# A layer in one core: modulation in plain f32 by column groups, x loaded first, values in 512 columns

## The reference

```python
mod_ctx = jax.nn.silu(c_ctx)[None, :] @ w_mod[l] + b_mod[l]      # 1024 -> 6 * 1024
mod_lat = jax.nn.silu(c) @ w_mod[l] + b_mod[l]
...
shift1, scale1, gate1, shift2, scale2, gate2 = [m[:, None, :] for m in jnp.split(mod, 6, axis=-1)]
h = _rmsnorm(x, g_norm1) * (1 + scale1) + shift1
proj = h @ w_in + b_in
q_raw, k_raw, v_raw, o_raw, gates, u_pool, g_a, g_b = jnp.split(proj, split_at, axis=-1)
y_a, C, n, m = _mlstm_branch(q_raw, k_raw, v_raw, o_raw, gates, gn_gain, C0, n0, m0)
...
x = x + gate1 * (merged @ w_out)
h2 = _rmsnorm(x, g_norm2) * (1 + scale2) + shift2
x = x + gate2 * _hier_moe(h2, ...)
```

## Time and profile before

| | before |
|---|---|
| median of 3 runs | 1079.4 us (1077.72 to 1080.03) |
| the profiled execution | 1075.08 us |
| its span, first to last instruction | 1073.3 us |
| mean granted clock of PE, as a share of 2.4 GHz | 0.965 |
| PE busy | 993.5 us, 93% |
| DVE busy | 634.5 us, 59% |
| ACT busy | 515.3 us, 48% |
| POOL busy | 133.7 us, 12% |

### The profile page before, as it was taken

How to read it: one execution, slowest core, us unless ns; L and a number is a source line. 1 busy time by engine, 2 the same in 40 slices (tenths; PEclk the granted TensorE clock), 3 DMA queues, 4 the chain that set the end, 5 groups by cost and what they waited for, 6 DMA issues and landing times.

```text
span 1073.3 us, 14490 instructions
## 1 busy us (share of the span) xinstructions
PE 993.5 (93%) x5934; PEld 873.2 (81%) x5934; DVE 634.5 (59%) x774; ACT 515.3 (48%) x656; POOL 133.7 (12%) x135
## 2 busy tenths in 40 slices
PE   6899999999999999999999999982999999999970
PEld 2378888899888989999998998882788888888860
DVE  0645643323476768232116444536699999999987
ACT  2353343413556664222214123223578787878763
POOL 3000000000110100896000000001011111111010
PEclk9899999999999999999999999985899999999995
DMA  9734434421334324231221124521899999999955
GB/s 348 312 118 176 176 135 184 157 105 40 89 93 119 92 57 156 107 126 66 79 79 67 56 75 182 229 94 64 360 379 416 422 411 417 413 419 416 396 231 203
DMA packets 36066, 216.41 MB, mean 202 GB/s; under 512 B 4352, under 2 KB 4800, under 8 KB 15520
## 3 DMA queue, kind: packets, MB, share of 16 engines
q1 hardware_dynamic: 27024, 180.23, 43.2%
q0 software_dynamic: 8112, 32.53, 8.7%
q10 hardware_dynamic: 864, 2.73, 0.6%
HBM read 200.68 MB, written 14.79 MB: 201 GB/s over the span
## 4 chain that ended last, share of the span: by engine, by line
PE 84%; DVE 6%; DMA 5%; ACT 2%; issue 1%; SPq 0%; DVEq 0%; POOL 0%; ACTq 0%; POOLq 0%
PE ps L1476 81%; DMA rowA<-yscr 2%; DMA raw<-in_wst 1%; PE ps L1857 1%; DVE xr L1454 1%; DVE rowB L1451 1%; DVE hn L958 1%; PE ps L1875 1%; DMA xg<-h2scr,slot_rows 1%; DVE hlo L971 0%; DVE hn L976 0%; DVE xr L1458 0%; PE ps L1808 0%; DMA yscr<-yb,slot_rows 0%; PE ps L1740 0%
## 5 line engine op out<-in xcount | busy, mean ns | idle before, releaser
L932 DVE TENSOR_TENSOR wlo<-raw,whi 128x2048 fp32r<-128x2048 f32 x37 | 86.1, 2329 | 146.9 <-ACT whi L579 146.9
L1476 PE MATMUL ps<-hhi,whi 128*128 128x320 f32 x672 | 153.9, 310 | 1.7 <-ACT gF L616 1.7
L1476 PE MATMUL ps<-hlo,whi 128*128 128x320 f32 x672 | 153.1, 309 | 0.0
L1476 PE MATMUL ps<-hhi,wlo 128*128 128x320 f32 x672 | 153.0, 309 | 0.0
L1476 PEld LDWEIGHTS ps<-hhi,whi 128*128 128x128 f32 x672 | 112.6, 188 | 4.9 <-ACT gF L616 2.0
L1476 PEld LDWEIGHTS ps<-hhi,wlo 128*128 128x128 f32 x672 | 112.4, 188 | 0.0
L1476 PEld LDWEIGHTS ps<-hlo,whi 128*128 128x128 f32 x672 | 112.4, 188 | 0.0
L579 ACT ACTIVATE whi<-raw 128x2048 fp32r<-128x2048 f32 x37 | 70.5, 1907 | 85.9 <-PE ps L1476 83.7
L1351 DVE TENSOR_TENSOR wlo<-raw,whi 128x2048 fp32r<-128x2048 f32 x32 | 72.6, 2289 | 5.4 <-ACT whi L859 5.3
L1351 DVE TENSOR_TENSOR olo<-raw,ohi 128x2048 fp32r<-128x2048 f32 x32 | 72.5, 2288 | 4.5 <-ACT ohi L859 4.5
L859 ACT ACTIVATE whi<-raw 128x2048 fp32r<-128x2048 f32 x32 | 61.3, 1919 | 18.3 <-PE ps L1476 18.3
(11 more groups left out here) (331 smaller groups left out, 2253.1 us busy)
## 6 DMA issues: line engine op xcount, KB each, us to landing
raw<-in_wexp SPq DMA_DIRECT2D x64, 1024.0 KB, 8.8
raw<-in_wst SPq DMA_DIRECT2D x60, 1024.0 KB, 5.0
eraw<-in_wexp SPq DMA_DIRECT2D x32, 1024.0 KB, 7.5
nm<-negscr POOLq DMA_DIRECT2D x8, 640.0 KB, 7.0
wib<-wiscr POOLq DMA_DIRECT2D x8, 512.0 KB, 6.1
xT<-in_x SPq DMA_DIRECT2D x4, 640.0 KB, 10.8
xr<-in_xt SPq DMA_DIRECT2D x1, 2560.0 KB, 10.9
h2scr<-ht ACTq DMA_DIRECT2D x5, 512.0 KB, 3.0
```

Of the source, the lines that this page charges most:

```text
L932: dve.tensor_tensor(lo[:, :], raw[s][:, :], f32(hi[:, :]), ALU.subtract)\
L1476: return nc.tensor.matmul(out, lhsT, rhs, start=start, stop=stop)
```

## The change

- `in_wst` is laid out anew for the modulation chunks and for the values. A modulation chunk of the start-up now holds four k tiles of 512 columns, these being shift and scale of two k tiles; so a pair of chunks (`i`, 0 to 3) completes shift1 and scale1 of k tiles 2i and 2i + 1.
- `mod_half` multiplies such a chunk straight from `raw`, in plain f32, in the start-up and in the query/key stage alike: four matmuls, one for each k tile, each with a stationary operand of 32 columns (`csil`, zeros beyond the first two) and with its own 32 rows of the result. `mod_columns` adds the four rows together as it transposes, by a constant with ones at rows 0 and 1 of each 32.
- The second modulation needs no split on ACT and DVE, and `wx`, `wxl`, `ch4`, `cz4` go. `split_no` gives the new count of splits.
- SP issues x first, then chunks; the eight small loads go to ACT's queue. `vb` is loaded after chunk AT_QK + 2.
- PE makes the sums of squares before any modulation matmul. DVE multiplies x by rstd at once, then takes the k tiles two by two as each pair's shift and scale arrive; query chunk 0 is split in the last of these turns.
- The gate matmuls of a k tile and those of query blocks 0 and 1 stand in one loop over k tiles, so the loop of 8 turns has no blocks left in turn 0, and waits there for the gates' copies.
- The values are made in two groups of 512 channels, each from two chunks of four k tiles: `value_block` multiplies 12 times 512 columns, and DVE adds 512 columns at a time, after the second chunk.
- POOL's memset of `Vt` and its loads wait for the last modulation chunk instead of `m_used`.

The diff, cut to its core:

```diff
+def split_no(c):
+    return 1 + (c - AT_QK) // 3 if c < AT_V else N_QK + 1 + c - AT_V
...
-        mrow1 = at("mrow1", 92, [4, 8 * P])
+        mrow1 = at("mrow1", TMP + 5, [P, 4, 512])
...
-        wx = at("wx", 152, [P, CH], F32R), at("wxl", 160, [P, CH], F32R)
-        QH, QL = whi + [wx[0]], wlo + [wx[1]]
-        ch4 = at("ch4", 177.75, [P, KT, 4], F32R)
-        cz4 = at("cz4", 178, [P, KT, 4], F32R)
+        QH, QL = whi, wlo
+        csil = at("csil", 176.75, [P, KT, 32])
...
-            smalls = [(cst[:, :], cst_d), (cin[:, :, :], c_d), (col[:, :], col_d),
-                      (wgr[:, :, :], wg_d), (bg[:, :], bg_d), (m0[:, :], m0_d),
-                      (wr[:, :, :], wr_d), (br[:, :], br_d)]
-            assert len(smalls) == N_SMALL
-            for dst, src in smalls:
-                sp.dma_start(dst, src).then_inc(d_const, 16)
+            for k in range(0, KT, 2):
+                sp.dma_start(xT[:, k:k + 2, :], x_d[:, k:k + 2, :]).then_inc(d_x[k // 2], 16)
...
-                if c < 4:
-                    sp.dma_start(xT[:, 2 * c:2 * c + 2, :], x_d[:, 2 * c:2 * c + 2, :])\
-                      .then_inc(d_x[c], 16)
-                elif c == 4:
+                if c == AT_QK + 2:
...
+            for dst, src in smalls:
+                act.dma_start(dst, src).then_inc(d_const, 16)
...
+            for i in range(4):
+                chunk_used(act, 2 * i + 1)
+                act.activation(mrow1[:, i, :], ps[:, 2 + i, :], ACT.Copy).then_inc(s_mrow, 1)
+                if i == 3:
+                    split_hi(AT_QK, QH[0])
+                for k in (2 * i, 2 * i + 1):
+                    act.wait_ge(s_hn, k + 1)
+                    act.activation(hhi[:, k, :], hn[:, k, :], ACT.Copy).then_inc(s_hhi, 1)
...
             for j in range(N_QK):
-                c = AT_QK + 3 * j
                 if j:
                     act.wait_ge(q_used, j)
-                split_hi(c + 1, QH[(j + 1) % 2])
-                if j:
-                    act.wait_ge(m_used, 2 * j)
-                split_hi(c + 2, QH[2])
+                split_hi(AT_QK + 3 * j + 3, QH[(j + 1) % 2])
                 block_qk(2 * j)
-                if j < N_QK - 1:
-                    act.wait_ge(m_used, 2 * j + 1)
-                    split_hi(c + 3, QH[(j + 1) % 2])
-                else:
-                    act.wait_ge(m_used, 2 * j + 1)
-                    split_hi(AT_V, QH[0])
                 block_qk(2 * j + 1)
                 mod_row2(j)
...
+            dve.wait_ge(s_rstd, 1)
+            for k in range(KT):
+                st.on(dve.tensor_tensor(hn[:, k, :], xT[:, k, :], rstd[:, :], ALU.mult))
...
+            for i in range(4):
+                dve.wait_ge(s_modT, i + 1)
+                both = mod[:, 0:16, :].rearrange("p (s k) c -> p s k c", s=2)[:, :, 2 * i:2 * i + 2, :]
+                bias = col[:, B_MOD:B_MOD + 16].rearrange("p (s k) -> p s k", s=2)
+                st.do(dve.tensor_tensor(both, ps[:, 0, 448 + 8 * i:456 + 8 * i].rearrange(
+                    "p (s k c) -> p s k c", s=2, c=2), by(bias[:, :, 2 * i:2 * i + 2].unsqueeze(3),
+                                                          [P, 2, 2, 2]), ALU.add))
+                st.do(dve.scalar_tensor_tensor(
+                    gain[:, 2 * i:2 * i + 2, :], mod[:, 8 + 2 * i:10 + 2 * i, :], 1.0,
+                    by(col[:, G_1 + 2 * i:G_1 + 2 * i + 2].unsqueeze(2), [P, 2, 2]), ALU.add, ALU.mult))
+                for k in (2 * i, 2 * i + 1):
+                    for c, a, b in ((0, 0, TC), (1, TC, T)):
+                        ins = dve.tensor_scalar(hn[:, k, a:b], hn[:, k, a:b], gain[:, k, c:c + 1],
+                                                mod[:, k, c:c + 1], ALU.mult, ALU.add)
+                    ins.then_inc(s_hn, 1)
+                if i == 3:
+                    split_lo(AT_QK, QH[0], QL[0])
+                for k in (2 * i, 2 * i + 1):
+                    input_lo(k)
 
...
             def splits_lo(j):
                 c, o = AT_QK + 3 * j, (j + 1) % 2
-                split_lo(c + 1, QH[o], QL[o])
-                split_lo(c + 2, QH[2], QL[2])
-                if j < N_QK - 1:
-                    split_lo(c + 3, QH[o], QL[o])
-                else:
-                    split_lo(AT_V, QH[0], QL[0])
+                split_lo(c + 3, QH[o], QL[o])
...
-            def value_rows(c, t):
-                n = c * NT + t
-                dve.wait_ge(v_ready, n + 1)
-                dve.tensor_tensor(Vt[:, t, 2 * c:2 * c + 2, 0:DH], ps[:, (n + 2) % 6, 0:2 * P].rearrange(
-                    "p (v n) -> p v n", n=P), vb[:, 2 * c * P:2 * (c + 1) * P].rearrange(
+            def value_rows(g, t):
+                u = g * NT + t
+                dve.wait_ge(v_ready, (2 * g + 1) * NT + t + 1)
+                dve.tensor_tensor(Vt[:, t, 4 * g:4 * g + 4, 0:DH], ps[:, (u + 2) % 6, :].rearrange(
+                    "p (v n) -> p v n", n=P), vb[:, 512 * g:512 * (g + 1)].rearrange(
                         "p (v n) -> p v n", n=P), ALU.add).then_inc(v_free, 1)
...
-            def mod_chunk(slot, use, out, c2):
-
-
-                pe.wait_ge(raw_full[slot], (use + 1) * 16)
-                for k in range(KT):
-                    last = mm(out, csil[:, k, 2 - 2 * c2:6 - 2 * c2],
-                              raw[slot][:, k * 2 * P:(k + 1) * 2 * P],
-                              k == 0 and c2 == 0, k == KT - 1 and c2 == 1)
+            def mod_half(c, kh, bank):
+
+                slot = raw_slot(c)
+                pe.wait_ge(raw_full[slot], (raw_use(c) + 1) * 16)
+                for kk in range(4):
+                    last = nc.tensor.matmul(
+                        ps[32 * kk:32 * kk + 32, bank, :], csil[:, 4 * kh + kk, :],
+                        raw[slot][:, kk * 512:(kk + 1) * 512], start=kh == 0, stop=kh == 1,
+                        tile_position=(0, 32 * kk))
                 last.then_inc(raw_free[slot], 1)
+
+            def mod_columns(rows, out):
+                for b in range(4):
+                    last = mm(out[:, 2 * b:2 * b + 2], rows[:, b * P:(b + 1) * P],
+                              cst[:, C_CMB:C_CMB + 2], True, True)
+                last.then_inc(s_modT, 1)
 
...
-            last.then_inc(s_modT, 1)
+            pe.wait_ge(s_csil, 3)
+            square_sums(hn, s_sum1, s_ssq)
+            for i in range(4):
+                mod_half(2 * i, 0, 2 + i)
+                mod_half(2 * i + 1, 1, 2 + i)
+                if i == 0:
+                    pe.wait_ge(s_rstd, 1)
+                pe.wait_ge(s_mrow, i + 1)
+                mod_columns(mrow1[:, i, :], ps[:, 0, 448 + 8 * i:456 + 8 * i])
 
             pe.wait_ge(s_wgl, 1)
+            chunk_split(AT_QK)
             for k in range(KT):
                 pe.wait_ge(s_hlo, k + 1)
                 last = three([(ps[0:GP, 6 + a, 0:HALF], cut_half(a)) for a in range(2)],
                              wgh[:, k, :], wgl[:, k, :], hhi[:, k, :], hlo[:, k, :],
                              k == 0, k == KT - 1)
-            last.then_inc(s_gps, 1)
+                if k == KT - 1:
+                    last.then_inc(s_gps, 1)
+                for b in range(2):
+                    o = (b * KT + k) * P
+                    last = three([(ps[:, 2 * b + a, 0:HALF], cut_half(a)) for a in range(2)],
+                                 QH[0][:, o:o + P], QL[0][:, o:o + P], hhi[:, k, :], hlo[:, k, :],
+                                 k == 0, k == KT - 1)
+                    if k == KT - 1:
+                        last.then_inc(q_ready, 1)
 
...
-            def mod_half(j, kh):
-                w = 2 if kh else (j + 1) % 2
-                chunk_split(AT_QK + 3 * j + 1 + kh)
-                if kh == 0:
-                    pe.wait_ge(s_mrow, 2 + j)
-                for kk in range(4):
-                    k = 4 * kh + kk
-                    mm(ps[0:4, 6, :], ch4[:, k, :], QH[w][:, kk * 512:(kk + 1) * 512], k == 0, False)
-                    last = mm(ps[0:4, 6, :], cz4[:, k, :], QL[w][:, kk * 512:(kk + 1) * 512], False,
-                              k == KT - 1)
-                last.then_inc(m_used, 1)
-
-            def mod_columns(i):
-                pe.wait_ge(s_mrow, 3 + i)
-                if i:
-                    pe.wait_ge(m_done, i)
-                for b in range(4):
-                    last = mm(ps[:, 7, 2 * b:2 * b + 2], mrow[:, b * P:(b + 1) * P],
-                              cst[0:4, C_CMB:C_CMB + 2], True, True)
-                last.then_inc(s_modT, 1)
-
-            pe.wait_ge(s_gate, 2)
-            pe.wait_ge(s_ch, 4)
             for j in range(N_QK):
-                block_q(j, 0)
                 if j:
-                    mod_columns(j - 1)
-                mod_half(j, 0)
-                block_q(j, 1)
+                    block_q(j, 0)
+                    pe.wait_ge(m_done, j - 1)
+                    pe.wait_ge(s_mrow, 4 + j)
+                    mod_columns(mrow, ps[:, 7, 0:8])
+                else:
+                    pe.wait_ge(s_gate, 2)
```

(60 more changed lines are left out.)

74 lines of the change are left out of this document (29 added, 45 removed).

## The result

The changed kernel takes 1084.38 us (median; 1081.38 to 1087.06), the kernel before 1079.24 us in the same rounds (1074.87 to 1080.22): ratio 1.0052, 95% interval 1.0033 to 1.0071, so it is slower by 5 us, and the forecast was 1086.7 us. The profiled execution took 1087.06 us, its span 1084.8 us.

What follows compares the result with a forecast made beforehand. PE was taken to bound the kernel, a chain of engines the start-up. Start-up +4.0, query/key +6.2, values -2.9 us gave +7.3 on the profiled 1075.1: 1082.4, or 1086.7 us on the median of 1079.4; range 1059 to 1099 us.

Steps and rivals of the forecast that it cites:

- the sum of +7.3 us: Whole kernel: start-up +4.0, query/key stage +6.2 and values -2.9 us, added to the profiled 1075.1 us.
- A half at 2.2 us: Modulation half on PE: only neighbouring groups' passes overlap, 2.2 us against 1.86 us before; fourteen halves +6.2 us with shape changes.
- Rival A: Modulation halves: groups wholly side by side, 0.88 us a half; ScalarE's order bounds the start-up; 1065.6 us; chance 0.25.
- the upper bound: Modulation half on PE: eight passes one after another, 3.5 us.
- 0.1 us for the change of shape: PE, query/key stage: 0.1 us added per half for changing between grouped and whole-array matmuls, bounds 0 and 0.3.
- Small loads at 8.6 us, bounds 7 and 11: Start-up DMA: the eight small loads on ScalarE's queue all landed by 8.6 us, bounds 7 and 11.
- POOL's sums, PE idle: Start-up: POOL's seven adds of 1.60 us end at 21.4 us; PE stands idle until then.
- ScalarE's order: Start-up: ScalarE copies pair 1's sums only after pair 0's high parts, costing 0.2 us, later pairs nothing.
- The merged loop: Gates and query blocks 0 and 1 on PE: 21.1 us plus 2.2 us slow clock, from 51.85 to 75.2 us.
- The stall at query chunk 1: End of start-up: PE waits 2.8 us for VectorE's split of query chunk 1, ready at 82.05 us.
- PE inside the turns: Query/key turns: PE doesn't wait, and the ScalarE and VectorE splits saved beside it give nothing.
- Values -2.9 us: Values on PE: 240 matmuls of 512 columns replace 480 of 256, 57.5 to 54.6 us.

Runs made afterwards that it cites:

- Experiment 4: Changed kernel with the four k tiles of a modulation half one after another in one column group, added in the same 32 rows: 1131.19 us, ratio 1.0484.
- experiments 1 and 2: 1: changed kernel, small loads back on SP's queue ahead of x, 1070.74 us. 2: kernel before, only small loads moved to ScalarE's queue, 1088.01 us.
- Experiment 5: Changed kernel with query chunk 1 split by ScalarE and VectorE before they take the gate sums: 1075.63 us, ratio 0.9973.
- experiment 9: Kernel before with only values in 512 columns, 1077.26 us; values back in 256 on the changed kernel, 1085.80 us, and on experiment 1's, 1073.22 us.
- experiment 1: Changed kernel with the eight small loads back on SP's queue, ahead of x: 1070.74 us, ratio 0.9925.
- experiment 3: Changed kernel with ScalarE squaring x before it waits for the small loads and does the tanh: 1070.59 us, ratio 0.9939.
- the last kernel of experiment 9: Kernel of experiment 1 with its values put back to 256 columns: 1073.22 us, ratio 0.9951.

## Why the prediction was right in its number and wrong in its reasons

The time lies 2.3 us from the forecast, inside the range and on the side given. But two large errors cancelled. Against the sum of +7.3 us, the trace has at the scores +6.8 us: +14.8 us of start-up not foreseen, +2.4 us of slow clock, -17.4 us in the halves (14 times 0.80 us saved, not 0.44 us lost), -0.3 us in the values.

- **A half at 2.2 us: wrong.** Rival A's price holds. The step that failed is that the two passes of one f32 matmul stand next to each other and so only one neighbour overlaps: four passes start at 107.1 us and four at 107.6 us. A half takes 1.0 us, 0.12 us more than the 0.88 us of rival A. Experiment 4 shows the other end, 3.6 us, as the upper bound had it. The Trainium skill ("TensorE: Matmul & The Clock Gate", Part 3, The mechanism) gives a group of matmuls one matmul's time and some 4 ns for each further tile. The trace agrees for each pass: four records start between 107.1 and 107.2 us, and the next four some 0.45 us later. The forecast had carried the same section's rule on strict order over to the two passes inside a matmul, which the page doesn't do and the trace contradicts.
- **0.1 us for the change of shape: right.** Of the turn of 17.25 us the columns take 0.88 us and two halves 2.0 us, so two blocks have 14.37 us, where they had 14.07 us. If the change of shape is all of that, it is 0.15 us for each half, inside the bounds.
- **Small loads at 8.6 us, bounds 7 and 11: wrong, the largest term.** 20.9 us. The step took the latency of an idle DMA (2.0 us behind the last issue) and added a little for bandwidth; the loads' bytes are few, and it was their packets that queued (experiments 1 and 2). What hung on it was seen (POOL's sums, PE idle), and those durations held: the adds took 11.58 us, against 11.2 us. The sums were done at 36.7 us, 12.7 us after their forecast, the last pair's columns at 62.1 us, 14.4 us after it, and the block of chunk 1 at 96.82 us, 14.8 us after it: PE's first instruction is 12.8 us late (34.22 us against 21.4 us), so most of the lag is there from the start.
- **ScalarE's order: right place, wrong size.** 0.2 us was put for the copy of the second pair behind the first pair's high parts. It was 3.95 us, because the second pair's halves were done 7.2 us after the sums of squares and not 10.6 us, while the high parts came when expected (10.6 us after them, against 10.7 us). It is the bound that rival A named. It then led into the slow clock, which made the third and fourth pair 3.64 us and the columns from the second pair on 1.87 us: some 4.4 us that neither the forecast nor a rival had.
- **The merged loop: right.** Predicted 21.1 us and 2.2 us of slow clock; 66.33 to 89.7 us is 23.4 us.
- **The stall at query chunk 1: right in kind.** 2.8 us by the forecast, 5 us by rival A, 5.14 us measured, plus the 2.4 us of slow clock that it set off, which no case had. Experiment 5 takes both away.
- **PE inside the turns: right.** No wait of PE after 96.82 us in this stage; a turn is fully busy. VectorE's and ScalarE's saved splits gave nothing there.
- **Values -2.9 us: right for the stage** (3.2 us), doubtful in the time (experiment 9).

Had the loads been at 8.6 us, the forecast's steps with the true half would have given rival A's 1065.6 us; experiment 1 measured 1070.7 us. Its loop starts at 54.19 us, 5.0 us after that rival's 49.2 us, and most of this is the slow clock: its columns follow each other every 6.16 us (35.75, 41.91 and 48.07 us), where the rival had 4.35 us and experiment 3 at full clock 4.32 us. The chances went wrong in one more way: A and late loads were weighed as alternatives, and they came together.

## What to carry to other kernels

Count a small load on a second queue in packets, not bytes: while another queue streams large packets, each of its packets waits for a large one. Issue what the first computation waits for ahead of the stream on the same queue, or let nothing but its true user wait for it. Where a stage gets shorter on one engine, look for the copy or split that was hidden behind it (3.95 and 5.14 us here), and count the slow clock that follows a gap as well (2.4 us behind one wait here, some 4.4 us behind the other). Don't explain the clock of one profile by an edit before two kernels with the same code there have been compared. And when a forecast has two uncertain terms of opposite sign, a right total proves neither.

## What the runs showed of the hardware

- Plain f32 matmuls of 32 columns in four column groups: sixteen passes of 512 columns in 1.92 us, against 7.05 us in one group, so 3.7 times as fast.
- Two DMA queues shared the engines packet for packet (350 and 351 in 6 us) at 2.22 and 0.25 MB.
- After a wait of PE of 3.95 us the granted clock stayed at 0.50 through two pairs of grouped halves, busy for 5.3 and 5.4 of 6 us; after a wait of 3.99 us (experiment 3) it was back at 1.00 after one such pair. Two kernels with the same start-up code differ in the same way: it stayed down behind a wait of 5.35 us (experiment 1) and came back behind one of 4.56 us (the last kernel of experiment 9).
